# Cross-attention output by token chunks, routing of six tiles under the last chunk, row stores on ScalarE's queue

## The chip, the cores and the metric

The kernel runs on one core of a Trainium2 chip. TensorE (PE) multiplies, VectorE (DVE), ScalarE (ACT) and GpSimd (POOL) work elementwise, and SyncE (SP) issues most of the DMAs. One launch computes everything. The metric is the device time in microseconds of one launch; lower is better.

## The reference

Two layers run over 1024 prompt tokens and 32 sample tokens (8 sequences of 4), 1056 tokens in all, with width 1024. All arithmetic that matters here is float32. Each layer has a token mixer, a cross attention and a mixture of 32 experts. The part that the change touches is the end of the cross attention and the start of the experts:

```python
x = x + y                                       # token mixer
x = x + (o @ w_xo)                              # o: cross attention, 512 wide
h = rmsnorm(x, g_ffn)
g_logit = h @ w_rg + b_rg                       # 4 groups
g_sel = argmax(g_logit)
e_logit = (h @ w_re + b_re)[the 8 experts of g_sel]
top_p, top_i = top_k(softmax(e_logit), 2)
gates = softmax(g_logit)[g_sel] * top_p / sum(top_p)
# rows are sorted by expert; every block of rows runs one expert
hid = silu(rows @ w_eg[e]) * (rows @ w_eu[e])
out = hid @ w_ed[e]
x = x + sum over the two experts of gates * out[its row]
```

The outputs are the normed tokens of both streams and the caches and states of both layers.

## The kernel before

The activations x lie in SBUF transposed: 128 partitions by 8 slices of the width by 1056 tokens. Tokens come in nine tiles: eight of 128 and one (tile 8, NT) of 32. A loop over the two layers runs on each engine, and the engines meet only at semaphores and at five stage ends (`stage_end`: each of PE, ACT, DVE and POOL drains, counts `stage_done` up, and waits for all four; SP isn't in it). Nothing plans the work: each engine runs what its function writes down, in that order.

The stretch in question, in order:

- `x_out(j, c)` (L1381): for each of the 8 slices j of the width, and each of three chunks c of 352 tokens, four 128x128 weights give a product in PSUM (L1392). After each j, VectorE adds 1056 columns to x (L2522), ScalarE writes x times the gain into xn (L1869) and the squares (L1870), VectorE sums the squares (L2507), and `logits(j - 1)` (L1403) multiplies xn by the router's weight of 36 columns (4 groups and 32 experts), which is the stationary side; the 352 tokens stream.
- After the last slice PE sums the squares over the partitions, tile by tile (L1422, one column each, 18 instructions), counts up `ssq_ready`, and turns the 36xtokens logits into tokens x 36 (L1427). SP waits for `ssq_ready` before it loads the gate and up weights of experts 2 and 3 (`load_gu`, L669, 2 MB each, for four of the five buffers can be filled ahead).
- `rows_of(t)` (L1437) turns tile t of xn back into rows, ScalarE scales and copies them (L1886) into four buffers `xr`, and SP stores them to DRAM as `xrow` (L684), 512 KB a tile, on the same queue as the weights. Tile 4 and later need a buffer whose store has landed (`row_moved`).
- VectorE picks the group and the two experts of every token over all nine tiles at once (L2533 to L2564), sums the picks (`both`, L2570), and PE counts them per expert (L1445, L1447). VectorE turns the counts into a slot for each token and expert. `place`, an expert's rank by load, comes from a 32x32 comparison (L2577, L2578). Two rounds of one-hot tables follow (L2615 to L2621), whose products on PE (L1457) give the table of rows per block, and VectorE writes it as `idx` (L2629).
- POOL waits for all row stores and `idx`, gathers the rows of blocks 0 and 1 (L2874), and goes to the stage end. VectorE then works out the order of the experts (`order_i`, L2632 to L2635), the gates and the overflow list (L2637 to L2647), counts up `routed`, and goes to the stage end (L489).
- `keep_clock(bank, n)` issues n matmuls on constants (two PE instructions each, L777) so that PE has work. The one ahead of the first one-hot product has n = 36 and stands right behind `rows_of(8)`.
- The expert stage runs 22 blocks of 128 rows. A block takes four groups of 32 rows; an expert has two to four groups. Per block PE runs `gate_up` (L1484), the turn of the next block (L1470, `turn_x`) and `down` (L1508). SP loads 3 MB per expert through five pairs of buffers: `load_gu` when the block that used the buffer last is through, `load_dn` likewise. Ahead of that loop SP waits until both first gathers have landed, loads expert 4's gate and up weights, waits for `routed`, and loads expert 4's down weights.

## Time and profile before

| | |
|---|---|
| median of 3 runs | 2490.47 us (2487.63 to 2491.78) |
| the profiled execution | 2477.46 us |
| its span | 2475.7 us |
| granted clock, mean | 0.979 |
| PE busy | 2301.5 us (93%) |
| DVE busy | 1168.0 us (47%) |
| ACT busy | 657.2 us (27%) |
| POOL busy | 480.7 us (19%) |
| DMA | 390.82 MB, mean 158 GB/s |

The launch takes 1.8 us more than the span of its instructions. PE is busy nearly all the time, yet keep_clock's matmuls count as busy, so the share says little of the routing stretch: there the chain of waits is what to read. Times in the rows below are from the span's start. The first layer's cross output begins at 824 us, its first expert product at 942 us; the second layer's first expert product is at 2160 us. The share of the DMA engines is near 1 in the slices of both expert stages.

### The profile page before, as it was taken

How to read it: one execution, taken by the hardware profiler on the slowest of the kernel's cores; microseconds unless marked ns; L12 is line 12 of the kernel's file. 1: busy time of each engine (PE TensorE's matmuls, PEld its weight loads, DVE VectorE, ACT ScalarE, POOL GpSimd, SP SyncE). 2: the span in 40 equal slices, each digit the busy share in tenths (PEclk: the TensorE clock that was granted, in tenths of full speed). 3: DMA queues.
4: the chain of work that ended last, by engine and by line, in shares of the span. 5: the costliest groups of instructions: out<-in, count | busy, mean ns of one | idle time of the engine just before them, and what ended most of it. 6: DMA issues, size and time to landing. Idle time of an engine off the chain costs nothing.

```text
span 2475.7 us, 41476 instructions
## 1 busy us (share of the span) xinstructions
PE 2301.5 (93%) x17596; PEld 1359.3 (55%) x17596; DVE 1168.0 (47%) x2072; ACT 657.2 (27%) x1404; POOL 480.7 (19%) x590
## 2 busy tenths in 40 slices
PE   8999998889999999999899999988799999999984
PEld 5644565656666664333366456666566675733332
DVE  2455556874232354333263655568742342633334
ACT  1023554422012230111130335544220032211113
POOL 6003423520100001111260034235100000011113
PEclk9999999989999999999999999999899999999997
DMA  5001001163142148999840010011621411799996
GB/s 196 11 20 28 15 12 44 44 247 133 36 164 86 68 163 328 406 422 423 335 142 11 20 30 12 12 44 47 257 88 44 154 69 68 270 358 410 423 415 258
DMA packets 80288, 390.82 MB, mean 158 GB/s; under 512 B 20942, under 2 KB 25164, under 8 KB 60588
## 3 DMA queue, kind: packets, MB, share of 16 engines
q1 hardware_dynamic: 61948, 309.38, 32.5%
q0 software_dynamic: 17568, 76.57, 8.1%
q8 instruction: 143, 2.34, 0.4%
q10 hardware_dynamic: 576, 2.10, 0.2%
q14 instruction: 53, 0.43, 0.1%
HBM read 355.31 MB, written 41.41 MB: 160 GB/s over the span
## 4 chain that ended last, share of the span: by engine, by line
PE 76%; DVE 9%; issue 5%; ACT 3%; PEld 2%; DMA 2%; POOL 1%; POOLq 1%; PEldq 1%; SPq 0%; ACTq 0%; DVEq 0%
PE ps L1484 13%; PE ps L801 9%; PE ps L824 8%; PE ps L1508 6%; PE ps L1392 5%; PE ps L972 5%; PE ps L892 5%; PE ps L1192 3%; PE ps L984 2%; PE ps L950 2%; PE ps L1000 2%; PEld ps L824 2%; DVE arena L2225 2%; PE ps L1470 2%; PE ps L1214 1%
## 5 line engine op out<-in xcount | busy, mean ns | idle before, releaser
L1484 PE MATMUL ps<-arena 128*32 128x512 f32 x2304 | 316.9, 602 | 22.6 <-issue 16.8
L824 PE MATMUL ps<-arena,ring 128*128 128x352 f32 x936 | 277.9, 459 | 1.0 <-ACTq L489 1.0
L801 PE MATMUL ps<-x,ring 128*128 128x352 f32 x768 | 231.6, 463 | 11.1 <-DMA x<-in_x 9.6
L824 PEld LDWEIGHTS ps<-arena,ring 128*128 128x128 f32 x936 | 177.7, 190 | 99.4 <-ACTq L489 1.2
L2654 DVE COPY arena<-ps 128x1024 f32<-128x1024 f32 x44 | 53.9, 1224 | 336.9 <-PE ps L1470 336.9
L801 PEld LDWEIGHTS ps<-x,ring 128*128 128x128 f32 x768 | 146.9, 192 | 93.2 <-issue 13.3
L1484 PEld LDWEIGHTS ps<-arena 128*32 128x32 f32 x2304 | 92.4, 111 | 187.1 <-issue 187.1
L1508 PE MATMUL ps<-arena 128*32 128x512 f32 x1408 | 160.2, 595 | 3.8 <-ACT arena L1901 3.8
L2874 POOL DMA_INDIRECT arena<-xrow,arena x46 | 46.8, 1017 | 591.5 <-DVE arena L2629 319.9
L972 PE MATMUL ps<-arena 96*128 96x512 f32 (+3 forms) x384 | 144.9, 487 | 0.0
L1392 PE MATMUL ps<-arena,ring 128*128 128x352 f32 x384 | 117.7, 463 | 1.6 <-DVE arena L2487 1.6
L1484 PE MATMUL ps<-ring,arena 128*32 128x512 f32 x512 | 116.0, 607 | 0.0
L1670 ACT ACTIVATE ring<-ps 128x512 f32<-128x512 f32 (+2 forms) x192 | 87.7, 489 | 104.1 <-PE ps L984 104.1
L892 PE MATMUL ps<-arena,x 128*128 128x512 f32 x256 | 112.9, 601 | 2.2 <-ACT arena L1618 2.2
L1192 PE MATMUL ps<-arena 64*32 64x256 f32 x2560 | 90.2, 414 | 24.1 <-DVE arena L2359 15.1
L1675 ACT ACTIVATE ring<-ps,nmax 128x128 f32<-128x128 f32 (+7 forms) x128 | 94.7, 740 | 57.8 <-DVE nmax L2128 56.8
L2359 DVE STREAM_TRANSPOSE arena<-arena 128x1024 f32<-128x1024 f32 x80 | 95.9, 1227 | 24.4 <-PE ps L1192 23.1
L1896 ACT ACTIVATE arena<-ps 128x256 f32<-128x256 f32 x44 | 16.9, 383 | 329.1 <-PE ps L1484 329.1
L984 PE MATMUL ps<-consts,ring 128*128 128x128 f32 x576 | 89.7, 281 | 12.9 <-ACT ring L1670 6.5
L2127 DVE TENSOR_REDUCE nmax<-ps 128x1 f32<-128x128 f32 (+7 forms) x128 | 97.0, 758 | 4.4
L2126 DVE TENSOR_TENSOR ps<-ps,consts 128x128 f32<-128x128 f32 x128 | 38.2, 299 | 127.6 <-PE ps L972 126.5
L1392 PEld LDWEIGHTS ps<-arena,ring 128*128 128x128 f32 x384 | 71.7, 190 | 46.1 <-issue 6.8
(470 smaller groups left out, 3661.9 us busy)
## 6 DMA issues: line engine op xcount, KB each, us to landing
arena<-in_w_gu SPq DMA_DIRECT2D x52, 2048.0 KB, 14.3
arena<-in_w_dn SPq DMA_DIRECT2D x64, 1024.0 KB, 11.1
ring<-in_ring SPq DMA_DIRECT2D x56, 512.0 KB, 3.6
ring<-in_w_gu SPq DMA_DIRECT2D x12, 2048.0 KB, 13.9
arena<-yrow SPq DMA_DIRECT2D x16, 1024.0 KB, 9.3
arena<-in_mem_k SPq DMA_DIRECT2D x16, 512.0 KB, 7.2
arena<-in_mem_v SPq DMA_DIRECT2D x16, 512.0 KB, 9.2
xrow<-arena SPq DMA_DIRECT2D x16, 512.0 KB, 8.5
```

The costliest lines, as they stand in the source:

```text
L801: mm = pe.matmul(ps[:, PIECE_BANKS[n % len(PIECE_BANKS)], 0:CH], ring[:, j % RING, k, :], x[:, k, tok], start=k == 0, stop=k == KT - 1)
L824: mm = pe.matmul(ps[:, (j % 2) * NCH + c, 0:CH], ring[:, j // per, (j % per) * units + k, :], src[:, k, tok], start=k == k0, stop=k == uni ...
L892: mm = pe.matmul(ps[:, 6 + t % 2, :], x[:, k, t * P:t * P + m], wvg[:, k, :], start=k == 0, stop=k == KT - 1)
L972: mm = pe.matmul(ps[:, bank + at // 512, 0:end - at], q_h[0:QK, b, qb * P:(qb + 1) * P], k_h[0:QK, b, at:end], start=True, stop=True)
L984: mm = pe.transpose(ps[:, bank, (kb % 4) * P:(kb % 4 + 1) * P], prob[:, e, kb * P:(kb + 1) * P], ident)
L1192: mm = pe.matmul(ps[ND * g:ND * (g + 1), 4 + 2 * (n % 2) + h, 256 * x:256 * (x + 1)], q8[b][x][r, n, :], ct[r, m % NCT, 8 * g:8 * (g + 1), ...
L1392: mm = pe.matmul(ps[:, (j % 2) * NCH + c, 0:CH], ring[:, slot, (j % 2) * XH + k, :], co[:, k, tok], start=k == 0, stop=k == XH - 1)
L1484: mm = pe.matmul(ps[r, 2 + n % 2, :], xb_t[:, n % 2, k, r], w_gu[e % NW][:, k, :], start=k == 0, stop=k == KT - 1, skip_group_check=True)
L1508: mm = pe.matmul(ps[r, 4 + f, :], h_t[:, k, r], w_dn[e % NW][:, k, f * 512:(f + 1) * 512], start=k == 0, stop=k == 1, skip_group_check=True)
L1675: act.activation(prob[:, e, 0:w], ps[:, 2 * e:2 * e + 2, :].rearrange("p a n -> p (a n)")[:, 0:w], ACT.Exp, bias=nmax[:, e, 1:2], scale=ML ...
L2127: step(dve.reduce_max(nmax[:, e, 0:1], sc, AX))
L2359: dve.transpose(ct[:, m % NCT], keys).then_inc(ct_ready, 1)
```

## The change

The cross output runs by three token chunks of whole tiles: tiles 0 to 2, 3 to 5 (384 columns each), and 6 to 8 (288 columns), `XO_TILES`. The 24 units (chunk, slice) run in that order through three PSUM banks. Logits are computed with xn as the stationary side: for each unit and each of its tiles a 128x128 weight and 36 columns, so they come out as tokens x 36 and aren't turned. Six tiles (`EARLY`) are routed while the last chunk runs: their norms after slice 3 of it, and their group, first and second expert beside slices 4 to 6. Counting is split in the same way. `place` comes from a product on PE over the experts' comparisons. VectorE's stage end moves up to right behind `idx`; the order of experts follows it, and the gates and the overflow list (with `routed`) stand behind block 0's `hidden`. ScalarE issues the stores of the rows itself, each after its copy. keep_clock's counts change; the one of 36 stays.

```diff
+XO_TILES = ((0, 3), (3, 6), (6, NT + 1))
+XO_COLS = tuple(slice(a * P, min(b * P, TOK)) for a, b in XO_TILES)
+XO_UNITS = tuple((c, j) for c in range(len(XO_TILES)) for j in range(XO_MT))
+XO_BANKS = 3
+EARLY = XO_TILES[2][0]
...
-                sp.wait_ge(lin_done, IN_N + OUT_MT + XK_MT + XQ_MT + 1)
+                sp.wait_ge(xo_done, 1)
                 load_gu(0, 0)
                 load_gu(1, 1)
-                sp.wait_ge(ssq_ready, 2 * NCH + 1)
+                sp.wait_ge(ssq_ready, 2 * NCH + 2)
                 load_gu(2, 2)
                 load_gu(3, 3)
-                for t in range(NT + 1):
-                    m = P if t < NT else ND
-                    sp.wait_ge(xr_evac, t + 1)
-                    sp.dma_start(xrow[t * P:t * P + m, :], xr[0:m, t % 4, :]).then_inc(row_moved[t % 4], 16)
-
+                sp.wait_ge(xr_evac, NT + 1)
...
+                def logits(u):
+
+                    c, k = XO_UNITS[u]
+                    pe.wait_ge(xg_ready, u + 1)
...
+                    for t in range(*XO_TILES[c]):
+                        m = P if t < NT else ND
+                        mm = pe.matmul(ps[0:m, 3 if t < EARLY else 4, t * NR:(t + 1) * NR], xn[:, k, t * P:t * P + m], w_r[:, k, :],
+                                       start=k == 0 and t in (0, EARLY), stop=k == KT - 1, skip_group_check=True)
...
+                for u in range(len(XO_UNITS)):
+                    x_out(u)
+                    if u == 0:
+                        x_back(NT)
+                    if u >= 1:
+                        logits(u - 1)
+                    if XO_UNITS[u] == (2, 2):
+                        pe.wait_ge(sq_added, NCH + 1 + 2)
+                        token_sums(0, EARLY)
+                keep_clock(3, 4)
+                pe.wait_ge(sq_added, NCH + 1 + 3)
+                token_sums(EARLY, NT + 1)
+                logits(len(XO_UNITS) - 1)
...
-                for t in range(6):
+                for t in range(5):
                     rows_of(t)
-
-                keep_clock(5, 9)
                 pe.wait_ge(part_or_counts_ready, len(PART) + 1)
...
+                count_tiles(0, EARLY, 0)
+                rows_of(5)
+                pe.wait_ge(part_or_counts_ready, len(PART) + 2)
+                count_tiles(EARLY, NT + 1, 1).then_inc(ranked, 1)
+                count_above(0, EARLY)
+                count_above(EARLY, NT + 1).then_inc(ranked, 1)
+                keep_clock(3, 3)
+                pe.wait_ge(beaten_or_hot_ready, 1)
+                pe.matmul(ps[:, 2, 0:NE], ones[0:NE, :], beaten[0:NE, :], start=True, stop=True).then_inc(ranked, 1)
                 for t in range(6, NT + 1):
                     rows_of(t)
...
-                keep_clock(3, 34)
+                keep_clock(3, 22)
                 stage_end(pe, 9)
...
                     act.activation(xr[0:m, t % 4, :].rearrange("p (a n) -> p a n", a=2), ps[0:m, b:b + 2, :], ACT.Copy,
                                    scale=rstd_t[0:m, t:t + 1]).then_inc(xr_evac, 1)
+                    act.wait_ge(xr_evac, t + 1)
+                    act.dma_start(xrow[t * P:t * P + m, :], xr[0:m, t % 4, :]).then_inc(row_moved[t % 4], 16)
...
+                for u in range(len(XO_UNITS)):
+                    add_out(u)
+                    if u >= 1:
+                        add_xsq(u - 1)
+                    if XO_UNITS[u] == (2, 3):
+                        dve.wait_ge(std_ready, 2 * NCH + 1)
+                        step(dve.reciprocal(rstd_t[:, 0:EARLY], rstd_t[:, 0:EARLY]))
+                        dve.sem_inc(norm_ready, 1)
+                        dve.wait_ge(lg_done, 1)
+                        take_logits(0, EARLY, 3)
+                    elif XO_UNITS[u] == (2, 4):
+                        pick_group(0, EARLY)
+                    elif XO_UNITS[u] == (2, 5):
+                        first_of_max(e_all, NE, 0, EARLY, m1, oh1)
+                    elif XO_UNITS[u] == (2, 6):
+                        pick_second(0, EARLY)
+                        step(count_picks(0, EARLY))
...
-                step(dve.tensor_tensor(beats, key.unsqueeze(1).broadcast_to([P, NE, NE]), key.unsqueeze(2).broadcast_to([P, NE, NE]), ALU.is_gt))
-                step(dve.tensor_reduce(place, beats, AX, ALU.add))
+                step(dve.tensor_tensor(key_own[0:NE, :], key[0:NE, :], ident[0:NE, 0:NE], ALU.mult))
+                step(dve.tensor_reduce(key_col[0:NE, :], key_own[0:NE, :], AX, ALU.add))
+                dve.tensor_scalar(beaten[0:NE, :], key[0:NE, :], key_col[0:NE, 0:1], None, ALU.is_lt).then_inc(beaten_or_hot_ready, 1)
+                dve.wait_ge(ranked, 3)
...
+                stage_end(dve, 9)
+
                 by_place = place.unsqueeze(1).broadcast_to([P, NE, NE])
...
                     hidden(n)
+                    if n == 0:
+                        weigh_and_spill()
```

The order of instructions shows the three places. First PE at the end of the cross output, here of the kernel before: products of two slices of the width (L1392), each with the logits of the slice before it (L1403), then keep_clock (L777).

```order
L1392 MATMUL ps<-arena,ring 128x352 [waits lin_evac,ring_full3]
L1392 MATMUL ps<-arena,ring 128x352 x11
L1403 MATMUL ps<-arena 36x352 [waits xg_ready]
L1403 MATMUL ps<-arena 36x352 x2
L1392 MATMUL ps<-arena,ring 128x352 [waits lin_evac]
L1392 MATMUL ps<-arena,ring 128x352 x11
L1403 MATMUL ps<-arena 36x352 [waits xg_ready]
L1403 MATMUL ps<-arena 36x352 x2
L777 MATMUL ps<-consts 128x128 x5
L1403 MATMUL ps<-arena 36x352 [waits xg_ready]
L1403 MATMUL ps<-arena 36x352 x2
L777 MATMUL ps<-consts 128x128 x4
```

And in the changed kernel, units (2, 1) to (2, 3) of the last chunk, with the sums of six tiles' squares (L1414) between them:

```order
L1393 MATMUL ps<-arena,ring 128x288 [waits xo_added]
L1393 MATMUL ps<-arena,ring 128x288 x3
L1405 MATMUL ps<-arena 128x36 [waits xg_ready]
L1405 MATMUL ps<-arena 128x36
L1405 MATMUL ps<-arena 32x36
L1414 MATMUL ps<-consts,arena 128x1 [waits sq_added]
L1414 MATMUL ps<-consts,arena 128x1 x5
L1393 MATMUL ps<-arena,ring 128x288 [waits xo_added]
L1393 MATMUL ps<-arena,ring 128x288 x3
L1405 MATMUL ps<-arena 128x36 [waits xg_ready]
L1405 MATMUL ps<-arena 128x36
L1405 MATMUL ps<-arena 32x36
```

Each unit is four products of 288 columns and three logits, one for each tile, where one slice had twelve products of 352 columns and three logits of 352 streamed columns.

Second SP ahead of the expert stage; `xb_full` are the first gathers, L684 the stores of rows. Before:

```order
L669 DMA arena<-in_w_gu 128x4096 [waits ssq_ready]
L669 DMA arena<-in_w_gu 128x4096
L684 DMA xrow<-arena 128x1024 [waits xr_evac] x8
L684 DMA xrow<-arena 32x1024 [waits xr_evac]
L672 DMA arena<-in_w_dn 128x2048 x4
L669 DMA ring<-in_w_gu 128x4096 [waits xb_full1,xb_full0]
L672 DMA arena<-in_w_dn 128x2048 [waits routed]
```

After:

```order
L674 DMA arena<-in_w_gu 128x4096 [waits ssq_ready]
L674 DMA arena<-in_w_gu 128x4096
L677 DMA arena<-in_w_dn 128x2048 [waits xr_evac]
L677 DMA arena<-in_w_dn 128x2048 x3
L674 DMA ring<-in_w_gu 128x4096 [waits xb_full1,xb_full0]
L677 DMA arena<-in_w_dn 128x2048 [waits routed]
```

The nine stores are gone from SP, and what follows them waits for ScalarE's last copy instead. On ScalarE each store is issued right behind its copy, once the copy is complete, and ahead of the next copy.

Third VectorE from `idx` (first row) to the first blocks of the experts: `order_i`, then the gates and `over_i` (whose semaphore is `routed`), then xb's copy to SBUF. Before:

```order
L2629 CAST arena<-arena 128x92 [waits dve_step]
L2632 TENSOR_TENSOR arena<-arena 128x1024
L2633 TENSOR_TENSOR arena<-arena 128x1024 [waits dve_step]
L2634 TENSOR_REDUCE arena<-arena 128x32 [waits dve_step]
L2635 CAST order_i<-arena 128x32 [waits dve_step]
L2637 TENSOR_REDUCE arena<-arena 128x9 [waits rx_out,dve_step]
...
L2645 TENSOR_REDUCE arena<-arena 128x24
L2646 TENSOR_SCALAR arena<-arena 128x24 [waits dve_step]
L2647 CAST over_i<-arena 128x25 [waits dve_step]
L484 ISA
L2654 COPY arena<-ps 128x1024 [waits tx_done,stage_done]
```

After:

```order
L2706 CAST arena<-arena 128x92 [waits dve_step]
L2711 TENSOR_TENSOR arena<-ps,arena 128x1024 [waits stage_done]
L2712 TENSOR_TENSOR arena<-arena 128x1024 [waits dve_step]
L2713 TENSOR_REDUCE arena<-arena 128x32 [waits dve_step]
L2714 CAST order_i<-arena 128x32 [waits dve_step]
L2733 COPY arena<-ps 128x1024 [waits tx_done,dve_step]
...
L2742 TENSOR_TENSOR arena<-ps,arena 128x256 [waits dve_step]
L2719 TENSOR_REDUCE arena<-arena 128x9 [waits rx_out]
...
L2728 TENSOR_SCALAR arena<-arena 128x24 [waits dve_step]
L2729 CAST over_i<-arena 128x25 [waits dve_step]
L2733 COPY arena<-ps 128x1024 [waits tx_done]
```

The stage end (the wait for `stage_done`) moved from behind `over_i` to the row behind `idx`, and the ten instructions that end in `over_i` moved from ahead of block 0 to behind its last step (L2742).

## Rows read from the trace of the kernel before

**Rows 1.** Chain of waits, 893 to 1000 us: start us, us, what.

```profile
896.98 1.97 PE ps L1422 x18
...
904.19 13.94 DMA xrow<-arena
...
918.21 1.12 ACT arena L1886
...
919.38 1.05 PE ps L1437 x8
920.43 8.04 PE ps L777 x72
...
932.05 0.21 DVE arena L2629
...
940.86 1.24 DVE arena L2654
```

**Rows 2.** Timeline of PE: start us, us, engine line op out<-in xcount.

```profile
883.22 1.37 PE L1403 MATMUL ps<-arena 128*36 128x352 f32 x6
884.53 7.37 PE L1392 MATMUL ps<-arena,ring 128*128 128x352 f32 x24
891.82 1.37 PE L1403 MATMUL ps<-arena 128*36 128x352 f32 x6
```

**Rows 3.** Timeline of SP, the weight and row transfers it issues.

```profile
898.98 1.60 SPq L669 DMA_DIRECT2D arena<-in_w_gu  x2
901.89 20.26 SPq L684 DMA_DIRECT2D xrow<-arena  x9
...
939.58 0.33 SPq L672 DMA_DIRECT2D arena<-in_w_dn  x1
949.52 9.82 SPq L669 DMA_DIRECT2D arena<-in_w_gu  x2
```

**Rows 4.** Timeline of ACT: the table load ahead of the square roots.

```profile
896.78 1.28 ACT L1876 ACT_TABLE_LOAD   x1
```

**Rows 5.** One DMA issue on ScalarE: ns min/median/max.

```profile
L1840 ACTq DMA_DIRECT2D out_mv<-arena x1: 345/345/345, 716.0 to 716.0; - x1
```

**Rows 6.** Timeline of DVE in the routing.

```profile
901.64 0.20 DVE L2550 TENSOR_TENSOR arena<-arena 128x36 f32<-128x36 f32 x1
...
909.20 0.46 DVE L2570 TENSOR_TENSOR arena<-arena 128x288 f32<-128x288 f32 x1
911.08 0.82 DVE L2573 TENSOR_TENSOR_SCAN ring<-ring,ps 128x320 f32<-128x320 f32 x1 [1.42 <-PE ps L1445]
...
912.18 1.23 DVE L2577 TENSOR_TENSOR arena<-arena 128x1024 f32<-128x1024 f32 x1
...
928.68 1.36 DVE L2621 TENSOR_TENSOR ring<-arena 128x1152 bf16<-128x1152 f32 x1
```

**Rows 7.** DMA queues, 719 to 720 us: packets, MB, share of 16 engines.

```profile
q1 hardware_dynamic: 49, 0.20, 51.1%
q10 hardware_dynamic: 50, 0.20, 50.1%
```

**Rows 8.** DMA queues, 901 to 903 us.

```profile
q1 hardware_dynamic: 44, 0.72, 89.0%
```

**Rows 9.** DMA issues, 918 to 920 us: KB each, us to landing.

```profile
xrow<-arena SPq DMA_DIRECT2D x2, 512.0 KB, 4.3
```

**Rows 10.** Windows: PE, PEld, DVE, ACT, POOL busy (x), PEclk, DMA share, GB/s.

```profile
950.00:962.00 12.00, 10.59 (x97) 4.22 (x99) 5.91 (x8) 0.73 (x2) 1.97 (x2) 1.00 0.73 257
962.00:974.00 12.00, 12.00 (x114) 4.22 (x110) 4.35 (x6) 1.75 (x3) 2.04 (x2) 1.00 0.91 339
986.00:998.00 12.00, 12.00 (x114) 4.16 (x110) 4.34 (x6) 1.75 (x3) 2.03 (x2) 1.00 0.95 352
1178.00:1190.00 12.00, 8.65 (x68) 2.85 (x64) 0.80 (x2) 1.02 (x1) 1.02 (x1) 0.86 1.01 419
```

**Rows 11.** Chain of waits, 2100 to 2240 us, the second layer.

```profile
2134.52 3.53 PE ps L1437 x16
```

262 lines of the change are left out of this document (138 added, 124 removed).

## The prediction

> **What bounds the kernel now.** PE is busy 93% of the span, but in the routing much of that is keep_clock. So I read the chain of waits first, from the last cross product to the first expert block, then each engine's timeline there, then the DMA queues, and last the windows of the expert stage.
>
> The chain [rows 1] leaves the routing arithmetic. The sums of squares end at 898.95 us, and SP at once issues 4 MB of gate and up weights [rows 3]. The row stores stand behind these in the same queue: the store of tile 2, issued at 904.19, lands 13.94 us later, at 918.13. ScalarE's copy of tile 6 waits for that buffer (1.12), PE turns tile 8 (1.05, end 920.43), then come keep_clock's 72 matmuls (8.04), the one-hot products, and `idx` at 932.05. From the end of `rows_of(8)` to `idx` it is 11.62 us of fixed work. VectorE's second one-hot table is ready at 930.04 [rows 6], so VectorE is only some 0.6 us off the path. Behind `idx` the copy for block 0 starts 8.8 us later, at 940.86.
>
> The expert stage ends on transfers: at 1178 to 1190 us the DMA share is 1.01 while PE is busy 8.65 of 12 us at a granted clock of 0.86 [rows 10]. Before 974 us the engines have idle time: 0.27 of 12 us and 0.09 of 12.
>
> I work in the first layer and double it. All is set against the profiled execution, 2477.46 us, of which the span is 2475.7; the median shown is 13 us above it, and I add the same difference to both.
>
> **Cross output, on PE.** The products stay the same work: 8 x 1056 columns, 7.29 us a slice [rows 2]. The logits do not. Before, three of 352 columns take 1.31 us a slice (883.22 to 884.53), and six slices' worth stand ahead of the last product. After, each tile costs two instructions with a 128x128 weight and 36 columns. The trace does not show 36 columns; it shows 1 column at 1.97 / 18 = 0.109 us an instruction and 128 columns at 8.04 / 72 = 0.112 us [rows 1], so 36 cost between these: I take 0.109. Units 0 to 21 stand ahead of the last product: 22 x 6 x 0.109 = 14.4 us, less 6 x 1.31 = 7.9, plus 12 sums of the early tiles, 1.3: +7.8 us. The narrow tile 8 and the first unit, which needn't wait for the last tile, give some back: I take +7, so the last product ends at 898.8 instead of 891.8.
>
> **Routing under the last chunk, on VectorE.** A unit of it takes PE about 2.0 + 0.6 us. VectorE's pieces, from 0.20 us for 36 elements and 0.46 for 288 [rows 6]: each unit 0.9 for x and the squares. Unit (2, 3) must also wait for ScalarE: 0.5 for the addition, two copies of 0.4, the table load of 1.28 [rows 4], which before lay in a gap, a root of 0.2, then 1.0 for six tiles: 3.8 in all. Units (2, 4), (2, 5), (2, 6) come to about 3, 3 and 4. That is 13.8 against 10.4 us on PE, so VectorE is 3.4 us late at the last product. The rest to the late sums is 0.5 + 0.4 + 0.5 + 0.6 = 2.0. They end at 898.8 + 5.4 = 904.2, **5.2 us later** than now, and with them SP's two weight loads. The picks of the last three tiles, smaller, end 11.8 us behind the last product instead of 17.8: at 910.6 instead of 909.66 [rows 6].
>
> **Counts and place.** PE reaches the late count only behind `rows_of(5)`, which needs ScalarE's fourth copy. ScalarE starts its copies about 905.7 and now needs 1.12 + 0.35 for the issue [rows 5] + 0.1 a tile, so the fourth ends at 911.5 and the count near 912.7: the scan starts 1.7 us later than at 911.08. Place saves 2 x 1.23 [rows 6] and costs three small steps and a trip to PE, about 1.1: -1.4. Second table: 930.3 instead of 930.04. So VectorE alone would let `idx` come 0.3 us earlier (the floor).
>
> **Row stores on ScalarE's queue.** Store 0 is issued at 907.2 and store 2 at 910.3, while the 4 MB (from 904.2) flow. Bounds: in one line with the weights store 2 would again land 19.2 us behind SP's issue, +5.2. With nothing beside it a store lands in 4.3 us [rows 9]; then `rows_of(8)` ends at ScalarE's pace, near 917.2, or -3.2. Between: two hardware queues with 4 KB packets each get half, 49 and 50 packets in a microsecond [rows 7], so they take turns by packet. But the weights' packets are 0.72 MB / 44 = 16 KB [rows 8], the rows' 4 KB, so the stores get a fifth until the weights are through. The weights end about 917 with store 0 and a third of store 1 moved; the rest follows at full rate, and store 2 lands near 922.2. Of the old order only store 3 (1.3 us), which was in flight beside it, drops out: **+4.1**, which I take. Half the bytes would give +1.4. The page DMA: Bandwidth & Descriptors of the Trainium skill says in its section Issuing engines are not separate DMA queues that issuing from several engines saves only issue time, as all run on the same 16 DMA engines. By that alone the sum here would have +5.2 instead of +4.1; its section Queues, rings and completion order, which has the engines take turns between rows of queues packet by packet, agrees with the split of rows 7.
>
> So `rows_of(8)` ends at 924.5, and `idx` comes 4.1 us later. VectorE's earlier routing is not on the path.
>
> **Barrier behind idx.** The stage end now opens when PE's 44 remaining keep_clock matmuls (4.9 us from the table) and POOL's two gathers are through: 3.9 us behind `idx`. The order of experts (three passes of 1.23 and a cast, 3.9) follows it, ahead of block 0's copy. That makes 8.0 us instead of 8.8: -0.8. The four waits saved are small because the same 3.9 us stand behind the barrier. The cover of the gather (both had landed before 939.58 [rows 3]) is enough.
>
> **routed behind block 0.** SP waits for it with expert 4's down weights, and expert 5's gate and up weights stand behind that wait. Now they go at 939.58 and 949.52 [rows 3]. After, `routed` follows block 0 (7.1), a copy, `hidden` (3.0) and 3.3 of its own: about 956.9, so expert 5 goes 8 us later. 3 MB at 0.41 MB/us are 7.6 us of transfers moved out; of the idle time behind 957 they take back 2.4 + 1.1 and 0.05 x 12 = 0.6 [rows 10]. If the stage's end hangs on transfers alone, it is 7.6 - 4.1 = 3.5 later. If on PE's start, it is 0.8 earlier. Rows 10 point to transfers, but later loads are released at PE's pace and there are five buffers: I take the middle, **+1.4**, which contains the -0.8.
>
> Sum: (4.1 + 1.4) x 2 = 11 us. 2477.5 + 11 = 2488.5 for the profiled run, and 2490.5 + 11 = **2501.5** for the median.
>
> **Rivals.**
> - *The stores come free.* If a ring of its own lets stores through at near 4.3 us each, VectorE's table decides: front -0.3, and with the hold hidden -0.8: 2 x -1.1 = -2 us, **2488.5**. For it: rows 7. Against: those packets were of equal size. It decides if store 2 lands before about 917.5. 20%.
> - *Faster.* The same, and VectorE keeps up with PE in the last chunk (the 3.4 us of lag do not arise). The second table is then some 3 us earlier: 2 x -3.8, **2483**. For it: VectorE is busy 47% only. Against: the sum of its steps. 13%.
> - *The clock.* PE idles for 4 us or more ahead of `rows_of(6)`. In the second layer the same spot already runs at half speed: 16 turns in 3.53 us instead of 1.75 [rows 11]. If rows and part of the 72 matmuls run at 1.2 instead of 2.4 GHz in the first layer, +3.7, in the second some 2 more: **2507**. 12%.
> - *The hold counts in full*: +3.5 instead of +1.4, **2505.5**; 8%. *Hidden*: -0.8, **2497**; 7%. *One line for all transfers*: +5.2, **2503.5**; 4%.
> - The forecast itself: 36%.
>
> Slower is then 36 + 12 + 8 + 7 + 4 = 67%, the same (within 0.2%, 5 us, what a measurement of this kernel can tell) 20%, faster 13%. The range leaves the faster case out and cuts the clock's: 2486.5 to 2508. The forecast's own: 2496 to 2506.
>
> **What would show it.** Right: the logits at 0.109 us an instruction, last product 7 us later behind the start of the cross output; late `ssq_ready` 5 us later; store 2 landing about 12 us behind its issue; 11.6 us from `rows_of(8)` to `idx`; the copy for block 0 8.0 us behind `idx`; expert 5's weights issued 17 us behind the first turn of block 0; then a DMA share near 1 from 958 us. Wrong: stores of 5 us or less beside the 16 KB packets, a late sum no later than now, or experts that end no later although their loads do.

## The result: 26 us slower, more than twice the forecast

| | before | after |
|---|---|---|
| median of 4 runs each, same chip | 2489.55 us (2487.63 to 2491.78) | 2515.76 us (2513.97 to 2518.41) |
| profiled execution | 2477.46 us | 2517.42 us |
| its span | 2475.7 us | 2515.6 us |
| granted clock, mean | 0.979 | 0.967 |

The ratio is 1.0109, 95% interval 1.0096 to 1.0123: 26 us slower, where 11 were forecast and 2508 was the top of the range. The profiled execution of before was 12 us shorter than the median of its runs, so the two profiles differ by more than the kernels do. Part of that lies ahead of the change: the cross output starts at 824.43 us before and at 829.14 after. So from here on every time in a layer is counted from the first product of its cross output.

| us from the first cross product | before, layer 1 | layer 2 | after, layer 1 | layer 2 |
|---|---|---|---|---|
| last product ends | 67.5 | 67.5 | 75.6 | 75.6 |
| late sums end, SP issues the 4 MB | 74.5 | 74.5 | 80.8 | 80.8 |
| `rows_of(8)` ends | 96.0 | 96.5 | 103.3 | 103.2 |
| `idx` ends | 107.8 | 108.3 | 115.6 | 115.4 |
| stage end open, block 0 turned | 115.2 | 115.9 | 122.3 | 122.5 |
| copy for block 0 starts | 116.4 | 117.1 | 126.2 | 126.5 |
| block 0's `gate_up` ends | 124.9 | 125.5 | 136.2 | 136.2 |
| last `gate_up` of the expert stage ends | 380.2 | 381.2 | 395.2 | 397.4 |

The two layers agree. A layer's last `gate_up` ends 15 to 16 us later by the profiles; the medians leave 13 us a layer. Here is the path in the profile after. First the timeline of PE in the first layer (start us, us, engine line op out<-in xcount, idle time before it and what ended it):

```profile
908.73 1.21 PE L1414 MATMUL ps<-consts,arena 128*128 128x1 f32 x6 [2.24 <-DVE arena L2560]
...
911.12 5.97 PE L1456 MATMUL ps<-consts,arena 128*128 128x128 f32 x32
...
927.03 5.38 PE L1456 MATMUL ps<-consts,arena 128*128 128x128 f32 x24 [4.02 <-ACT arena L1926]
932.21 8.41 PE L778 MATMUL ps<-consts 128*128 128x128 f32 x72
...
951.40 1.09 PE L1492 MATMUL ps<-consts,arena 128*128 128x128 f32 x8 [2.74 <-POOLq L494]
956.74 8.64 PE L1506 MATMUL ps<-arena 128*32 128x512 f32 x64 [4.25 <-DVE arena L2733]
```

The late sums (908.73) take 1.21 us for 6 instructions, and the 24 of `rows_of(6)` to `rows_of(8)` 5.38 us, 0.22 us each: half speed. Both follow idle time, 2.24 and 4.02 us. The windows give the granted clock in the turns of tiles (last three columns: granted clock, DMA share, GB/s) as 0.50, the lower level of 1.2 GHz:

```profile
910.00:914.00 4.00, 4.00 (x20) 3.85 (x21) 2.64 (x17) 1.00 (x3) 0.00 (x0) 0.50 0.79 266
928.00:932.00 4.00, 4.00 (x21) 3.45 (x20) 3.65 (x14) 2.79 (x3) 0.00 (x0) 0.50 0.87 354
```

Before, a tile's 8 took 1.05 us [rows 1]. Block 0's `gate_up` takes 8.64 us instead of the 7.07 us of the kernel before, whose line is this:

```profile
942.23 7.07 PE L1484 MATMUL ps<-arena 128*32 128x512 f32 x64 [1.48 <-DVE arena L2654]
```

Next the chain of waits (start us, us, what):

```profile
914.34 11.45 DMA xrow<-arena
...
932.41 8.21 PE ps L778 x72
```

```profile
944.53 0.22 DVE arena L2706
...
945.64 1.10 POOL arena L2955
946.74 4.61 POOLq L494
...
951.38 1.24 DVE arena L2711
...
955.15 0.19 DVE order_i L2714
...
955.37 1.24 DVE arena L2733
```

Tile 0's store on ScalarE's queue takes 11.45 us beside the weights. Its landing frees the buffer for tile 4; the three last turns follow at half speed, and keep_clock's 8.21 us behind them. Then `idx` (944.53), a gather on POOL (945.64), and 4.61 us in which POOL's queue waits at the stage end. Only behind it come the order of experts (951.38 to 955.33) and the copy (955.37), 10.84 us behind the start of the `idx` cast; before it was 8.8 [rows 1]. Last, SP's issues:

```profile
909.97 0.80 SPq L674 DMA_DIRECT2D arena<-in_w_gu  x2
933.58 2.07 SPq L677 DMA_DIRECT2D arena<-in_w_dn  x4
951.29 0.33 SPq L674 DMA_DIRECT2D ring<-in_w_gu  x1
973.90 0.33 SPq L677 DMA_DIRECT2D arena<-in_w_dn  x1
975.30 1.47 SPq L674 DMA_DIRECT2D arena<-in_w_gu  x2
```

The two transfers that in [rows 3] went at 939.58 and 949.52 now go at 973.90 and 975.30: net of the 4.7 us at the start, expert 5's weights leave 21 us later, of which the later block 0 explains only 11.

### The profile page after: what moved, and what is told of

Its sections match the earlier page's. It is cut to its first block, busy times and chain, and to the rows that moved or that the text cites. A ratio compares the mean times of both kernels' runs of the same rounds, so it can differ in the third digit from the quotient of the medians.

```text
span 2515.6 us, 41790 instructions
## 1 busy us (share of the span) xinstructions
PE 2327.6 (93%) x17650; PEld 1386.4 (55%) x17650; DVE 1177.1 (47%) x2192; ACT 668.6 (27%) x1464; POOL 482.4 (19%) x590
## 4 chain that ended last, share of the span: by engine, by line
PE 74%; DVE 10%; issue 5%; ACT 3%; PEld 2%; POOL 2%; DMA 1%; POOLq 1%; PEldq 1%; SPq 0%; ACTq 0%; DVEq 0%
PE ps L1506 13%; PE ps L802 9%; PE ps L825 8%; PE ps L1530 6%; PE ps L973 5%; PE ps L893 5%; PE ps L1193 4%; PE ps L1393 4%; PE ps L985 2%; PE ps L951 2%; PE ps L1001 2%; PEld ps L825 2%; DVE arena L2267 2%; PE ps L1492 1%; PE ps L1215 1%
## 5 line engine op out<-in xcount | busy, mean ns | idle before, releaser
L825 PE MATMUL ps<-arena,ring 128*128 128x352 f32 x936 | 277.9, 459 | 1.0 <-ACTq L494 1.0
L825 PEld LDWEIGHTS ps<-arena,ring 128*128 128x128 f32 x936 | 177.7, 190 | 99.4 <-ACTq L494 1.2
L1393 PE MATMUL ps<-arena,ring 128*128 128x384 f32 (+1 forms) x384 | 125.3, 469 | 0.0
L1193 PE MATMUL ps<-arena 64*32 64x256 f32 x2560 | 100.0, 413 | 18.1 <-DVE arena L2401 12.8
L2168 DVE TENSOR_TENSOR ps<-ps,consts 128x128 f32<-128x128 f32 x128 | 38.3, 299 | 127.1 <-PE ps L973 126.1
L1949 ACT ACTIVATE arena<-ps 128x1024 f32<-128x1024 f32 x44 | 45.1, 1026 | 179.4 <-PE ps L1530 179.4
```

The source lines that it names most:

```text
L825: mm = pe.matmul(ps[:, (j % 2) * NCH + c, 0:CH], ring[:, j // per, (j % per) * units + k, :], src[:, k, tok], start=k == k0, stop=k == uni ...
L1193: mm = pe.matmul(ps[ND * g:ND * (g + 1), 4 + 2 * (n % 2) + h, 256 * x:256 * (x + 1)], q8[b][x][r, n, :], ct[r, m % NCT, 8 * g:8 * (g + 1), ...
L1393: mm = pe.matmul(ps[:, u % XO_BANKS, 0:tok.stop - tok.start], ring[:, slot, (j % 2) * XH + k, :], co[:, k, tok], start=k == 0, stop=k == X ...
```

## The experiments

All kernels are compared with the kernel before, run beside them on the same chip. It measured 2482 to 2490 us from chip to chip, so I compare ratios, and an expectation that names a time is read as a distance from the kernel before; the changed kernel itself, run again on another chip (a_ref), gave 2517.21 us against 2490.24, again 1.0109 [1.0094, 1.0125]. A name with a_ is an edit of the kernel after, b_ of the kernel before. Differences of 0.1% lie within the intervals and aren't read. From a_kcdn's 1.0089 to a_sp's 1.0127 every interval overlaps the changed kernel's, so what these edits do is read from their traces, and the time is named only beside it.

| kernel | ratio to before, 95% | us over before |
|---|---|---|
| after (and a_ref) | 1.0109 [1.0096, 1.0123] | 26 |
| b_act: stores alone | 0.9996 [0.9987, 1.0005] | -2 |
| b_tail: tail alone | 1.0066 [1.0053, 1.0079] | 16 |
| a_chunk: front alone | 1.0080 [1.0067, 1.0093] | 21 |
| a_tail: tail undone | 1.0079 [1.0062, 1.0096] | 18 |
| a_sp: stores undone | 1.0127 [1.0113, 1.0142] | 30 |
| a_drain | 1.0092 [1.0077, 1.0107] | 23 |
| a_hold | 1.0104 [1.0087, 1.0121] | 25 |
| a_clock | 1.0096 [1.0077, 1.0115] | 23 |
| b_gates3 | 1.0040 [1.0025, 1.0054] | 11 |
| b_late3 | 1.0066 [1.0047, 1.0085] | 15 |
| a_late3 | 1.0126 [1.0105, 1.0147] | 31 |
| a_kc | 1.0102 [1.0081, 1.0123] | 24 |
| a_dn | 1.0121 [1.0096, 1.0146] | 32 |
| a_kcdn | 1.0089 [1.0069, 1.0109] | 23 |
| b_best4 | 1.0007 [0.9991, 1.0022] | 0 |
| b_bestdn | 1.0001 [0.9988, 1.0015] | -1 |
| a_all | 1.0064 [1.0050, 1.0078] | 15 |

The last column is median less median.

### One part alone, one part undone

**b_act** moves the row stores to ScalarE's queue in the kernel before.

```diff
-                    sp.dma_start(xrow[t * P:t * P + m, :], xr[0:m, t % 4, :])...
+                    act.wait_ge(xr_evac, t + 1)
+                    act.dma_start(xrow[t * P:t * P + m, :], xr[0:m, t % 4, :])...
```

> The kernel before with the row stores alone moved to ScalarE's queue. Theory (a store waits for the 4 MB of weights whichever queue it is in): the first store lands within 2 us of where it landed from SP's queue, the last turn of a tile ends within 1.5 us of 96.0 us behind the start of the cross output, and the time is 2487 to 2493. Rival (a queue of its own lets the stores through): stores of 5 us, VectorE's second table sets idx, 2487 at the lowest, since only 0.6 us a layer is to be had. Second rival (the issue on ScalarE, 0.35 us a tile, delays its copies on the path): +1 to +3 us a layer, 2492 to 2496.

The queue hardly matters: in the first layer `rows_of(8)` ends at 95.2, `idx` at 107.4 (before 96.0 and 107.8), and the time is that of before. **a_sp**, the same undone in the kernel after, agrees.

> The kernel after with the row stores back on SP's queue, behind the weights of experts 2 and 3. Theory (as above, the queue hardly matters): 2514 to 2519. Rival (in a queue behind the 4 MB the stores land 19 us behind the issue of these, as before; in the kernel after the first lands 15.8 us behind it): the last turn of a tile ends 1 to 3 us a layer later, 2518 to 2522. Second rival (the issue on ScalarE costs): 2510 to 2513.

It is 1.0127, with an interval that overlaps the changed kernel's, at the theory's upper end and inside the first rival's range. But its last turn ends 0.1 and 0.8 us later than in the changed kernel, not 1 to 3, and its `idx` is at 115.5, where the changed kernel's is at 115.6.

**b_tail** is the kernel before with the new tail (a scratch table, `over_f`, lies at another address in it).

```diff
                 dve.tensor_copy(idx, table).then_inc(idx_ready, 1)
+                stage_end(dve, 9)
...
-                dve.wait_ge(rx_out, 1)
...
-                dve.tensor_copy(over_i[:, :], over_c).then_inc(routed, 1)
-                stage_end(dve, 9)
...
                     hidden(n)
+                    if n == 0:
+                        weigh_and_spill()
-                keep_clock(3, 34)
+                keep_clock(3, 22)
                 stage_end(pe, 9)
```

> The kernel before with the new tail alone: stage end right behind idx, order of experts behind it, gates and spill behind block 0, 22 instead of 34 keep_clock ahead of the stage end. Theory (the tail costs by itself what undoing it in the kernel after gave back, some 7 us): the copy for block 0 starts about 10.7 us behind idx instead of 8.6, the DMA share behind the start of block 0 falls to 0.15 to 0.3, and the time is 2496 us. Rival (the tail costs only together with the later front, since with an early front there is slack ahead of the transfers): 2489 to 2491. The prediction's own terms for this part alone (-0.8 to +3.5 a layer, doubled) give 2488 to 2496.

16 us, at which neither the theory nor the rival aimed: the tail alone costs more than the prediction's worst for it (+3.5 a layer). Its PE timeline, with the same columns as above:

```profile
935.68 5.14 PE L777 MATMUL ps<-consts 128*128 128x128 f32 x44
944.09 1.15 PE L1470 MATMUL ps<-consts,arena 128*128 128x128 f32 x8 [3.26 <-POOLq L489]
949.43 9.94 PE L1484 MATMUL ps<-arena 128*32 128x512 f32 x64 [4.19 <-DVE arena L2657]
```

PE waits 3.26 us for POOL's drain (`POOLq L489`) and 4.19 for the order of experts, and then runs block 0 in 9.94 us instead of 7.07, so that it ends 5.8 us later than in the kernel before. Behind it come `hidden`, the gates and `routed`, and then the weights of expert 5:

```profile
943.98 0.33 SPq L669 DMA_DIRECT2D ring<-in_w_gu  x1
967.89 0.33 SPq L672 DMA_DIRECT2D arena<-in_w_dn  x1
969.29 1.47 SPq L669 DMA_DIRECT2D arena<-in_w_gu  x2
```

**a_tail** is the reverse, the kernel after with the tail of before, and **a_chunk** has in addition the stores back on SP's queue, so that only the front is new.

> The kernel after, with the end of the routing on VectorE as before: the order of experts, the gates and the spill all stand ahead of the stage end. Theory (the new tail costs time, because POOL's drain at the stage end now waits in the open for its two gathers, and because expert 5's weights leave only behind block 0): the copy for block 0 starts about 8.8 us behind idx instead of 10.84, expert 5's weights are issued some 12 us earlier than in the kernel after, the window behind the start of block 0 has a DMA share above 0.5 instead of 0.15, and the time falls by 10 to 14 us, to about 2503. Rival (the front alone, the cross output with its half clock and the stores, holds the loss): the block 0 copy moves by 2 us, the stage end takes it back, and the time stays at 2512 to 2516.

> The kernel before with the new front alone: cross output by chunks of tokens and the routing of the early tiles under the last chunk, rows stored by SP, tail as before. Theory (the front by itself costs what remains when the tail is undone, +8 us in the last product of each layer, of which nothing is won back by the earlier start of the routing): 2505 to 2509, the last product 8.1 us later behind the start of the cross output, idx 7 to 8 us later. Rival (the front costs only together with the stores' queue): below 2498.

a_tail is 18 us above before, so undoing the tail gives back 8 to 9 us, less than the theory's 10 to 14 and more than its rival allows. The front alone costs 21 us, more than was expected. Its late sums end at 80.3, its `idx` at 114.9 and 115.2, its last `gate_up` at 389.8 and 391.1. The front and the tail, alone, add up to 37 us, together they cost 26. A part of the difference is that block 0 runs partly at half speed in both alone (9.12 and 8.68 us in a_chunk, 9.94 and 8.39 in b_tail) and only once in the changed kernel (8.64 and 8.36): about 5 us over both layers by the profiles.

### What opens the stage end

**a_drain** puts POOL's drain ahead of its gathers and leaves its wait behind them.

```diff
+                pool.drain().then_inc(stage_done, 1)
                 for n in range(2):
                     gather(n)
-                stage_end(pool, 9)
+                pool.wait_ge(stage_done, 4 * (BARRIERS.index(9) + 1))
```

> The kernel after, with POOL's drain and its signal ahead of the two gathers and only its wait for the others behind them. Theory (the drain waits for the gathers' landing, and the stage end opens 6.8 us behind idx for that alone): the stage end opens as soon as PE's keep_clock is through, some 5 us behind idx, the copy for block 0 starts about 9 us behind idx instead of 10.84, and the time falls by about 4 us, to 2512. Rival (the opening hangs on PE, which runs its keep_clock slowly, or the gathers themselves become later): no earlier than 6.8 us, no change in time.

```profile
944.46 0.21 DVE L2706 CAST arena<-arena 128x92 int32<-128x92 f32 x1
948.65 1.22 DVE L2711 TENSOR_TENSOR arena<-ps,arena 128x1024 f32<-128x1024 f32 x1 [3.98 <-PEq L494]
...
952.64 1.23 DVE L2733 COPY arena<-ps 128x1024 f32<-128x1024 f32 x1
```

The DVE timeline shows it: the stage end opens 4.0 us behind the cast of `idx` (944.46 to 948.65) and is now opened by PE (its bracket names `PEq`), not by POOL. The copy starts at 952.64, 8.2 us behind the start of the cast instead of 10.84, close to the 8.0 that the prediction gave. The stage end thus opens 2.7 us earlier, so POOL's drain was on the path. Block 0 then takes 9.53 us instead of 8.64, so that it ends only 1.4 us earlier, and the time falls by 3 to 4 us, within the two intervals. That the drain lasts until the gathers have landed is seen best in a_dn and a_late3 below: the second gather lands at 122.4 and 123.7 us, the stage end opens at 122.6 and 123.9.

**a_dn** and **a_kcdn** move the four down weights behind the landing of these gathers; **a_kc** shortens keep_clock ahead of the first one-hot product; a_kcdn has both.

```diff
-                for e in range(4):
-                    load_dn(e, e)
                 for p in range(2):
                     sp.wait_ge(xb_full[p], 16)
+                for e in range(4):
+                    load_dn(e, e)
...
-                    keep_clock(3, (36, 8)[s_])
+                    keep_clock(3, (14, 8)[s_])
```

> The kernel after with the four down weights (4 MB) issued behind the landing of block 0's and block 1's rows instead of ahead of them. Theory of the train (the gathers stand behind 4 MB of down weights on the DMA engines): the gathers land about 4.5 us behind idx instead of 6.6, the stage end opens some 4.9 us behind idx instead of 6.8, block 0's copy comes 1.9 us earlier a layer, and the time falls by 3 to 5 us against the kernel after. Rival (the length of POOL's drain is the gathers' own): stage end as before, no change in time.

> The kernel after with 14 instead of 36 keep_clock between the last turn of a tile and the product for the first one-hot table, in both layers. Theory (the 72 matmuls of 8.2 us stand on the path, since the second table is ready 4.5 us ahead of its product, so they turn the late rows into a late idx): idx comes 3 to 4 us earlier a layer, and the time is 2508 to 2510. Rival (TensorE falls to half speed for want of them, and block 0 with it): 2513 to 2518.

> The kernel after with both: 14 instead of 36 keep_clock ahead of the first one-hot product, and the down weights behind the gathers. Theory of the train: now the earlier idx (4.3 us) counts, since nothing stands ahead of the gathers; block 0's copy 6 us earlier a layer than in the kernel after, about 120 us behind the start of the cross output, and the time falls by 8 to 12 us. Rival (half speed of TensorE or the late down weights take it back): less than 6 us.

a_dn is a miss for the theory: with 4 MB fewer in the queue the stage end still opens 6.9 us behind `idx` (6.7 in the changed kernel). Two gathers take that long by themselves once `idx` is as late as here. In a_kc it is the other way: `idx` comes 4.4 us earlier (111.2), and the stage end opens 9.2 us behind it, only 1.9 us earlier than in the changed kernel. Block 0 ends 1.1 us earlier for it, and the time hardly falls (1.0102): the rival's time, though by the stage end rather than by the clock alone (block 0 takes 9.52 us). Its row on PE:

```profile
935.07 5.18 PE L778 MATMUL ps<-consts 128*128 128x128 f32 x44
945.48 1.93 PE L1492 MATMUL ps<-consts,arena 128*128 128x128 f32 x8 [5.23 <-POOLq L494]
```

The 4 MB of down weights had been issued behind the last row copy, and the gathers stand behind them. With both edits (a_kcdn) the 6.9 us are back and block 0's copy starts at 122.0 and 120.9, 4.3 and 5.6 us earlier than in the changed kernel; the time falls to 1.0089, 5 us, which is less than the theory's 8 to 12.

### Do the stores wait for the weights

**a_late3** and **b_late3** issue the weights of experts 2 and 3 behind the row stores. Here is the edit of a_late3:

```diff
-                load_gu(2, 2)
-                load_gu(3, 3)
                 sp.wait_ge(xr_evac, NT + 1)
+                load_gu(2, 2)
+                load_gu(3, 3)
```

> The kernel after with SP's loads of the gate and up weights of experts 2 and 3 behind the last copy of a tile, so that the row stores have no transfers beside them. Theory (the stores of 11.4 us beside the 4 MB hold tiles 6 to 8, and behind them idx): a store lands in about 4 us, the last turn of a tile ends 6 us or more earlier, VectorE's second table then sets idx, which comes 3 to 4 us earlier a layer, the weights come in time for blocks 2 and 3, and the time is 2507 to 2510. Rival (VectorE's late count and the slow clock hold idx whatever the stores do): idx moves by less than 1 us, 2514 to 2517. Second rival (the weights are missed): the expert stage grows by what the stores give.

> The kernel before with the gate and up weights of experts 2 and 3 issued behind its nine row stores. Theory (in the kernel before VectorE's tables are only 0.6 us off the path): stores of about 4 us, the last turn of a tile near 89 to 91 us behind the start of the cross output instead of 96.0, idx only 0.5 to 1 us earlier a layer, time 2487 to 2489. Rival (the weights issued some 12 us later delay the expert stage, which ends on transfers): 2492 or more.

In a_late3 the stores are then fast, `rows_of(8)` ends 6.2 us earlier (97.1 for 103.3) and `idx` 4.4. Both theories are a miss all the same: b_late3 is 15 us slower than before, as its rival had it, and a_late3 no faster than the changed kernel (1.0126 for 1.0109):

```profile
933.95 5.18 PE L778 MATMUL ps<-consts 128*128 128x128 f32 x44
947.95 1.97 PE L1492 MATMUL ps<-consts,arena 128*128 128x128 f32 x8 [8.82 <-POOLq L494]
```

PE is idle 8.82 us until POOL's drain ends, which is 10.70 us long instead of 4.61: the gathers now stand behind 8 MB, and the stage end opens 12.7 us behind `idx`. What the rows gain, the gathers lose. b_late3 shows the same, and one thing more. It issues the 4 MB 20 us later than the kernel before, and its first `gate_up` ends at 134.4 instead of 124.9, 9.6 us later; the weights of expert 5, the first that need a buffer back, leave with that end:

```profile
917.79 1.94 SPq L669 DMA_DIRECT2D arena<-in_w_gu  x2
...
957.98 9.82 SPq L669 DMA_DIRECT2D arena<-in_w_gu  x2
```

Its last `gate_up` is at 390.0, 9.8 us later than before: as much as block 0's end, and half of what the transfers were released later.

### The account: from the late sums to the last `gate_up`

From the late sums to the last `gate_up` a layer moves 118 to 121 MB in every one of these kernels, in 284 to 292 us of busy time of the DMA engines (their share summed over windows of 5 us, at most 1 in each). What differs is how long they are idle. The windows of the first layer from the late sums on: 50 us, 50 us, and the rest up to the last `gate_up`. The columns are window, its length, busy time of PE, PEld, DVE, ACT and POOL with counts, granted clock, DMA share, GB/s; before, then after, then a_all:

```profile
899.00:949.00 50.00, 42.64 (x373) 35.28 (x373) 36.21 (x96) 11.53 (x13) 3.19 (x3) 1.00 0.88 337
949.00:999.00 50.00, 48.59 (x444) 17.89 (x444) 19.88 (x25) 6.62 (x13) 8.06 (x8) 1.00 0.88 336
999.00:1205.00 206.00, 197.79 (x1762) 69.25 (x1754) 64.66 (x81) 29.04 (x50) 32.47 (x32) 0.98 1.00 415
```

```profile
910.00:960.00 50.00, 38.57 (x272) 33.54 (x276) 27.60 (x84) 11.75 (x13) 3.49 (x3) 0.81 0.83 316
960.00:1010.00 50.00, 48.59 (x443) 17.15 (x436) 19.18 (x30) 5.65 (x11) 7.08 (x7) 1.00 0.73 289
1010.00:1224.00 214.00, 202.82 (x1802) 70.98 (x1801) 68.45 (x85) 29.75 (x51) 33.58 (x33) 0.98 1.01 420
```

```profile
910.00:960.00 50.00, 38.76 (x275) 29.30 (x274) 27.50 (x84) 11.56 (x12) 3.09 (x3) 0.83 0.82 316
960.00:1010.00 50.00, 48.59 (x444) 17.93 (x444) 23.08 (x35) 6.78 (x13) 8.10 (x8) 1.00 0.93 356
1010.00:1216.00 206.00, 196.66 (x1758) 68.45 (x1750) 64.54 (x81) 28.98 (x51) 32.57 (x32) 0.98 1.00 414
```

In the rest the share is about 1 in all three: the expert stage is bound by its transfers there, at 414 to 420 GB/s. All the difference lies in the first 100 us. Before, the shares of 0.88 and 0.88 leave 12 us idle; after, 0.83 and 0.73 leave 22. The worst place in the kernel after lies around the end of block 0's `gate_up`, at 965.4 us:

```profile
957.00:965.40 8.40, 8.40 (x65) 2.24 (x58) 0.00 (x0) 0.00 (x0) 0.00 (x0) 0.82 0.16 66
965.40:974.00 8.60, 7.19 (x68) 3.15 (x72) 7.10 (x15) 0.39 (x1) 0.99 (x1) 1.00 0.17 44
```

Up to block 0's end the DMA engines have little to move, since five experts' buffers are filled ahead and the sixth load waits for block 0; behind it they wait for `routed`. In the kernel before their share while block 0 runs, 942.2 to 949.3 us, is 0.90, so there is little to win there.

Late sums plus busy time plus idle time is by its construction the time of the last `gate_up`, whatever the cause. For a given end of block 0, the idle time ahead of it shrinks by as much as the late sums come later, so this sum can't tell which of the two is paid for. The end of block 0's `gate_up` can. All in us from the first cross product of the layer:

| | late sums | block 0's `gate_up` ends | last `gate_up` | last less block 0's, layer 1 | layer 2 |
|---|---|---|---|---|---|
| before | 74.5 | 124.9 | 380.2 | 255.3 | 255.7 |
| b_act | 74.5 | 126.1 | 381.6 | 255.5 | 254.8 |
| b_best4 | 74.5 | 122.5 | 377.8 | 255.3 | 256.9 |
| b_late3 | 74.5 | 134.4 | 390.0 | 255.6 | 254.8 |
| a_chunk | 80.3 | 134.5 | 389.8 | 255.2 | 256.3 |
| a_tail | 80.3 | 134.6 | 390.5 | 255.9 | 255.2 |
| a_hold | 80.3 | 135.3 | 390.8 | 255.6 | 256.6 |
| a_all | 80.3 | 130.7 | 386.2 | 255.4 | 255.5 |
| b_gates3, held | 74.5 | 126.1 | 385.2 | 259.1 | 259.8 |
| b_tail, held | 74.5 | 130.7 | 390.2 | 259.5 | 259.4 |
| a_drain, held | 80.8 | 134.9 | 395.0 | 260.1 | 259.8 |
| after, held | 80.8 | 136.2 | 395.2 | 259.0 | 261.2 |
| b_bestdn | 74.5 | 122.2 | 381.0 | 258.8 | 256.2 |

Where expert 5's weights aren't held back (the first eight rows), the last `gate_up` ends 255 to 257 us behind the end of block 0's, in both layers, with late sums at 74.5 or 80.3 and block 0's end anywhere from 122.5 to 137. Where they wait for `routed` ("held"), it is 259 to 261, some 4 us more; the held runs outside the table have 258.9 to 260.2, but for 257.2 in the first layer of a_sp. So a later release counts only by what it does to block 0's end. b_bestdn stands apart: it moves the four down weights behind block 0's rows, so 6 MB are still on their way when block 0 ends (share 0.91 in the 8 us ahead of it and 1.03 in the 12 us behind it), and there the transfers, not block 0, are what counts.

The first layer's 15.0 us are then: `idx` 7.8 later, from `idx` to the first product of block 0 2.0 more, that block's `gate_up` 1.6 longer, and 3.7 for the hold. In the second layer they are 7.1, 2.3, 1.3 and 5.5.

**a_hold** and **b_gates3** are about the hold. In a_hold SP waits for the order alone and issues expert 5's weights ahead of expert 4's down weights (these must wait for `routed`, as their buffer holds the routing's scratch). b_gates3 is b_tail with the order of experts ahead of the stage end again:

```diff
-                stage_end(dve, 9)
                 by_place = place.unsqueeze(1).broadcast_to([P, NE, NE])
...
                 step(dve.tensor_copy(order_i[:, :], order_f))
+                stage_end(dve, 9)
```

and a_hold:

```diff
                 load_gu(4, 4)
-                sp.wait_ge(routed, 1)
-                load_dn(4, 4)
+                sp.wait_ge(ranked, 4)
...
                         load_gu(r % NW, e)
+                    if r == NW:
+                        sp.wait_ge(routed, 1)
+                        load_dn(4, 4)
...
                 step(dve.tensor_copy(order_i[:, :], order_f))
+                dve.sem_inc(ranked, 1)
```

> The kernel after, but SP waits only for the order of experts ahead of expert 5's gate and up weights, and for routed ahead of expert 4's down weights, which now stand behind expert 5's gate and up. Theory (transfers set the end of the expert stage): expert 5's weights leave right behind the products of block 0, about 10 us earlier than in the kernel after, the idle stretch of the DMA engines (share 0.15 in the 12 us behind the start of block 0) fills, and the time falls by 6 to 12 us, to about 2506. Rival (PE's later start sets the end, and the hold is hidden): within 3 us of 2515.8.

> The kernel before with the gates and the spill alone moved behind block 0; the order of experts stays ahead of the stage end, which stands between the two, and 22 instead of 34 keep_clock stand ahead of it. Theory (the hold of expert 5's weights costs about 4 us a layer in the expert stage, and the stage end comes 3.3 us of VectorE's work earlier, of which POOL's drain leaves about 1.3): block 0's copy 7.3 us behind idx instead of 8.6, the DMA share behind the start of block 0 about 0.15, the time 2493 to 2497. Rival (the hold is hidden, all of the loss of the new tail is its stage end in the wrong place): 2485 to 2488.

The trace of a_hold does what the theory says: the window behind block 0's end is filled,

```profile
956.00:1006.00 50.00, 48.59 (x443) 17.16 (x436) 19.17 (x30) 5.65 (x11) 7.08 (x7) 1.00 0.82 316
```

0.82 instead of 0.73, and the last `gate_up` is at 390.8 and 393.7 instead of 395.2 and 397.4. Its time doesn't show these 8 us: 25 us over before is in the rival's range, and its interval, 22 to 30 us, is too wide to deny half of them. That is open. b_gates3 shows the hold from the other side. Its block 0 starts no later than that of before (117.7 for 117.8) and ends 1.3 us later (8.46 us instead of 7.07), and behind that the stage takes 3.8 us more, 4.1 in the second layer. It is 11 us slower than before, where the theory had 3 to 7 and the rival none.

### The clock

**a_clock** has 13 instead of 4 keep_clock ahead of the late sums, 17 new ones behind the product for place, and 32 instead of 22 ahead of the stage end.

```diff
-                keep_clock(3, 4)
+                keep_clock(3, 13)
                 pe.wait_ge(sq_added, NCH + 1 + 3)
...
                 pe.matmul(ps[:, 2, 0:NE], ones[0:NE, :], beaten[0:NE, :], ...)
+                keep_clock(3, 17)
...
-                keep_clock(3, 22)
+                keep_clock(3, 32)
                 stage_end(pe, 9)
```

> The kernel after with more keep_clock where PE idles: 13 instead of 4 ahead of the late sums, 17 new ones behind the product for place, 32 instead of 22 ahead of the stage end. Theory (the idle gaps of 2.2 and 4.0 us let TensorE fall to half speed, and the half speed costs the turns of tiles and block 0): rows_of(6) to rows_of(8) take 2.7 us instead of 5.4 for 24 instructions, the late sums 0.6 instead of 1.2, idx comes 3 us earlier, and the time falls by 5 to 8 us, to about 2509. Rival (the stage hangs on the landing of the row stores and on ScalarE's copies): the turns get faster and idx stays, time within 3 us of 2515.8.

```profile
920.59 4.06 PE L778 MATMUL ps<-consts 128*128 128x128 f32 x34
925.02 1.10 PE L1456 MATMUL ps<-consts,arena 128*128 128x128 f32 x8 [0.36 <-ACT arena L1927]
...
954.44 9.62 PE L1507 MATMUL ps<-arena 128*32 128x512 f32 x64 [4.24 <-DVE arena L2734]
```

The turns run at full speed again, 8 in 1.10 us, `idx` comes 2.1 and 2.6 us earlier. Block 0 stays slow (9.62 us; PE is idle 4.24 us ahead of it, where this kernel has no keep_clock), so it ends 0.9 and 1.9 us earlier. The time falls by 3 to 4 us, less than the theory's 5 to 8 and within the two intervals.

Block 0's speed is not fixed by the kernel alone. In b_act, whose tail is that of before, its 64 products took 8.76 us in the first layer and 7.07 in the second, behind the same 1.48 us of idle time; in the profiled execution of before, 12 us shorter than the median, they took 7.07 in both. So the 1.6 us may in part belong to the execution.

### All of it behind the front

**a_all** keeps the front and has four edits behind it: the order of experts ahead of VectorE's stage end (as in b_gates3), and those of a_drain, a_hold and a_kc. It ran beside a_ref.

> The changed kernel itself, as the measure for the others on this chip: 1.0109 of the kernel before. Every theory expects the same.

> The changed kernel with its front untouched and four edits behind it together: 14 instead of 36 keep_clock ahead of the first one-hot product, order of experts ahead of the stage end, POOL's drain ahead of its gathers, expert 5's gate and up weights behind the order alone. Theory of the account (late sums plus idle DMA engines): the late sums stay 6.3 us later a layer than before, the added idle time of 9 us a layer falls to 1 to 3, and the time is 14 to 18 us above before and 8 to 12 below the changed kernel, a ratio to before of 1.006 to 1.007. Rival (block 0's start sets the end, since idx comes only 3.5 us later than before and block 0 starts some 3 us later than before): 5 to 8 us above before, a ratio of 1.002 to 1.003.

1.0064, 15 us over before, as the theory's numbers had it, and above the rival's 1.002 to 1.003. Yet it doesn't single out the late sums. They end 5.8 us later than before, and block 0's `gate_up` ends 5.9 us later (its copy starts 3.9 later, and it takes 8.99 us instead of 7.07); the last `gate_up` ends 6.0 us later. In the second layer the three are 5.8, 5.0 and 4.7: there block 0's end is the nearer. The two layers give 10.7 us of the 15; where the rest lies, these profiles don't show.

Three of the four edits, with the gates behind block 0, on the kernel before, without the shorter keep_clock (**b_best4**), and with the down weights moved too (**b_bestdn**):

> The kernel before with a tail put together from what the runs point to: order of experts ahead of the stage end, gates and spill behind block 0, POOL's drain ahead of its gathers, and expert 5's gate and up weights behind the order alone, ahead of expert 4's down weights, which wait for the spill. Theory (stage end, drain and hold are three separate costs): block 0's copy about 8 us behind idx, as its rows land 6.6 us behind idx in the train, expert 5's weights leave with the end of block 0's products, and the time is within 2 us of before, or 1 to 2 us below. Rival (the hold is not cured, as expert 4's down weights stay late): 4 to 10 us above before.

> The same, and the four down weights behind the landing of block 0's rows. Theory of the train: the rows land 4.5 us behind idx, block 0's copy starts 6 us behind idx instead of 8.6, and the time falls 3 to 6 us below before. Rival (the down weights are then missed by the first down products, or TensorE falls to half speed): at or above before.

```profile
931.77 5.14 PE L779 MATMUL ps<-consts 128*128 128x128 f32 x44
938.27 1.06 PE L1472 MATMUL ps<-consts,arena 128*128 128x128 f32 x8 [1.35 <-DMA arena<-xrow,arena]
940.81 7.07 PE L1486 MATMUL ps<-arena 128*32 128x512 f32 x64 [1.48 <-DVE arena L2659]
```

b_best4 is level with before, as expected; b_bestdn is a miss for its theory. In the first layer of b_best4 block 0's `gate_up` ends 2.4 us earlier than before, and the last `gate_up` ends 2.4 us earlier with it; in the second layer block 0 takes 9.98 us, ends 0.5 us later, and the gain is gone. In b_bestdn the first product is at 115.1 instead of 117.8 (940.81 less the start of 825.71), and the last `gate_up` at 381.0 instead of 380.2: the down weights, moved behind the rows, fill the DMA engines past block 0's end. No version beat the kernel before; b_act, b_best4 and b_bestdn are level with it.

## Why the prediction was wrong

The sign was right; the size failed, in these steps. The prediction had 5.5 us a layer, 4.1 for `rows_of(8)` and `idx` and 1.4 for all behind them; the profiles show 15.0 and 16.2, of which 7.8 and 7.1 are `idx` and 7 to 9 stand behind it.

- **Behind idx: an average instead of a sum.** This is the step that failed. The prediction had a gain of 0.8 us for the new stage end and a hold of 3.5 us if it counted in full, and took the middle of the two, +1.4. (Its 3.5 is 7.6 us of transfers moved out less 4.1 of idle time taken back. Of these, 2.4 stand in no row that it names; 957 to 962 us of the kernel before has a share of 0.48, which gives 2.6.) The runs show both as losses, one behind the other: +2.0 and +2.3 at the barrier and +3.7 and +5.5 for the hold, in b_gates3, which has the hold without the new barrier, 3.8 and 4.1. The rival in which the hold counts in full, at 8%, had this term.
- **Barrier behind idx.** -0.8 forecast, +2.0 and +2.3 measured. The opening was put at PE's keep_clock, 3.9 us behind `idx`; in a_drain it is 4.0. What was left out is that POOL's drain ends when its gathers land, and the stage end opens 6.7 us behind `idx`. Before, the order and the gates ran beside that.
- **routed behind block 0.** Expert 5's weights were to leave 17 us behind the first turn of block 0 and left 23.9 behind it: 2.8 of the difference are the order of experts ahead of the copy, which the prediction charged to the barrier alone, and 1.6 the slower block. The rest is `routed` itself, 10.0 us behind block 0's end where about 8 were forecast. In the 45 us behind that end the DMA engines are idle 8.4 us instead of 5.7, where a share near 1 was to be seen.
- **The front on the path.** +4.1 forecast, +7.3 measured at `rows_of(8)` and +7.8 at `idx`. The path was named rightly and mis-sized. The late sums are 1.1 us later than forecast, and the three last turns take 5.38 us at half speed; in a_clock, where they run at full speed, `rows_of(8)` ends 1.9 and 2.5 us earlier. (5.2 less 1.3 is 3.9, where the text has 4.1.)
- **The clock.** A rival, at +3.7 and 12%. It came in both layers, and also at a place not thought of: block 0, 8.64 instead of 7.07 us. The turns and block 0 together are some 3.5 us of the 15.
- **The last product.** +7 forecast, +8.1 measured. The logits cost 0.098 us an instruction (a unit's 6 in 0.59 us) where 0.109 was taken; in the last chunk, of three tiles with one short, a unit costs as much as any, and PE waits 0.75 us for ScalarE ahead of the first logits. **Late sums**: +5.2 forecast, +6.3 measured, of which 0.5 is half speed (80.3 where they ran at full speed).
- **Stores.** Tile 2's store was to land 12 us behind its issue and took 10.8. The number is near, the split that gave it is not, and that was luck: packets were to take turns, which gives the stores a fifth of the bytes. From 915 to 921 us, with stores under way beside the weights, they had a tenth (packets, MB, share; q1 carries the weights, q10 the stores):

```profile
q1 hardware_dynamic: 147, 2.15, 88.3%
q10 hardware_dynamic: 59, 0.24, 9.8%
```

The rest went behind the weights, which landed at 95.7 us, the first four stores at 96.6 to 100.3. For the time the queue didn't matter: b_act and a_sp show no effect, and a_late3 shows that faster stores bring nothing here. The Trainium skill, DMA: Bandwidth & Descriptors, says in its section Issuing engines are not separate DMA queues that a second issuing engine saves only issue time. The time of b_act agrees (0.9996), though its first four stores landed 0.5 to 2.1 us sooner than those of before.
- **Counts and place.** The scan starts 5.0 us later, not 1.7. The late count waits behind `rows_of(5)`, and this for ScalarE's fourth copy, which ended 2.8 us later than forecast: the late sums were 1.1 us later, and the last logits and the first turns ran at half speed. It stayed hidden: the second table is ready at 938.45, and its product runs at 942.91.
- **From rows_of(8) to idx.** 11.6 forecast, 12.1 measured, and it is not fixed work: 8.2 us of it is keep_clock, which a_kc cut to 3.5.

What stays open: why a_hold's time falls less than its trace, what makes block 0 slow in one execution and not in the next, and the rest of the 11 us by which front and tail together cost less than their sum. Each effect was read in single profiled executions, which lie up to 7 us from the median of their kernel (12 for the kernel before).

## What to carry to other kernels

In a stage that ends on transfers, look for the first load that needs a buffer back, and for what frees that buffer. If the DMA engines run idle ahead of it, its time is what counts: here the end of block 0's `gate_up` moved from 122.5 to 137 us, and the end of the stage moved with it, us for us. Loads released 20 us later cost nothing beyond what they did to that block. An account of idle and busy time shows where to look, but it adds up for any cause, so test it with an edit that moves one term and not the other. Terms behind one another are added, not averaged. A barrier moved forward uncovers every engine's drain; look which of them has a DMA in flight.

## What the runs showed of the hardware

- GpSimd's drain behind an indirect DMA lasted until the gather had landed: 4.61 us, 5.04 in the second layer, and 10.70 us with 8 MB of weights issued ahead of it (a_late3). There the second gather landed 0.2 us before the stage end opened.
- Two gathers of 128 rows of 4 KB had landed 6.7 and 6.8 us behind `idx` with next to nothing else in flight (a_dn), 8.9 us behind it with 4 MB issued ahead (a_kc) and 12.5 with 8 MB (a_late3).
- Tile 2's store of 512 KB, in packets of 4 KB beside 4 MB of weights, took 11.95 us on a second hardware queue (b_act) and 13.94 on the same [rows 1]; it landed 1.1 us sooner.
- A float32 product with 36 columns behind a 128x128 weight cost 0.098 us an instruction, one with 128 columns 0.112 [rows 1]: 3.6 times the columns for 14% more time.
- TensorE fell to half speed after idle times of 2.2 to 4.3 us in the routing, but not each time. 2.24 us ahead of the late sums gave 1.21 us for them in the changed kernel and 0.76 in a_tail, and in a_ref, the changed kernel run again, they end at 80.3 us in the first layer and at 80.8 in the second.
